# A streaming-encoder layer on one core: earlier input requests, squares folded further, memory operands and late taps moved in the engines' queues

## The reference

```
h = RMSNorm(x); split h @ w_in into q-latent, kv-latent, rope key, GLU input, gates A and B
yA = latent attention (16 heads, chunk-causal)        from the latents
yB = GLU -> causal depthwise conv, 31 taps -> LayerNorm -> swish -> @ w_pw2
x += (sigmoid(gA) * yA + sigmoid(gB) * yB) @ w_o
x += CrossAttn(RMSNorm(x), RMSNorm(mem))              4 heads, 256 memory tokens
x += SwiGLU(RMSNorm(x));  return RMSNorm(x)
```

## Time and profile before

| What | Value |
|---|---|
| timed runs, median (lowest to highest of 3) | 1681.59 us (1680.79 to 1682.99) |
| profiled execution, own time | 1683.29 us |
| its span, first to last instruction | 1681.1 us |
| TensorE busy | 1659.8 us, 99% |
| VectorE, ScalarE busy | 1111.0 and 826.2 us |
| mean granted TensorE clock | 0.997 |

### The profile page before, as it was taken

One profiled execution on the slowest core, in us unless ns is written; L12 is line 12 of the kernel. 1 busy time (PEld: TensorE's weight loads), 2 busy tenths in 40 slices (PEclk: granted clock), 3 DMA queues, 4 the chain that ended last, 5 costly groups with the idle time before them and its releaser, 6 DMA issues.

```text
span 1681.1 us, 23696 instructions
## 1 busy us (share of the span) xinstructions
PE 1659.8 (99%) x7728; PEld 1381.2 (82%) x7728; DVE 1111.0 (66%) x1414; ACT 826.2 (49%) x1049; POOL 102.0 (6%) x152
## 2 busy tenths in 40 slices
PE   8999999999999999999999999999999999999998
PEld 6888888888888888878888788888888888888886
DVE  5546777768987457885558856666666666654453
ACT  6555565555645444555544644444444444344343
POOL 3100010001000000120001200000000000000000
PEclk9999999999999999999999999999999999999999
DMA  6865555555665655554435566666666666565563
GB/s 209 260 200 163 175 157 164 153 166 159 183 212 182 197 191 175 181 192 157 150 133 174 189 196 193 191 186 187 196 200 198 190 193 193 189 223 188 176 213 136
DMA packets 160481, 309.67 MB, mean 184 GB/s; under 512 B 10256, under 2 KB 16400, under 8 KB 160176
## 3 DMA queue, kind: packets, MB, share of 16 engines
q1 hardware_dynamic: 158240, 301.50, 58.2%
q0 software_dynamic: 1488, 6.42, 1.1%
q10 hardware_dynamic: 704, 1.11, 0.2%
HBM read 306.89 MB, written 2.10 MB: 184 GB/s over the span
## 4 chain that ended last, share of the span: by engine, by line
PE 90%; DVE 4%; issue 3%; ACT 2%; DMA 1%; SPq 0%; DVEq 0%; ACTq 0%; POOLq 0%; POOL 0%
PE acc L357 27%; PE acc L359 27%; PE acc L358 27%; DVE w_lo L1247 2%; PE tp L369 1%; DVE x_f L1572 1%; ACT w_hi L772 1%; DMA raw<-in_w_in_dram 1%; PE acc L563 1%; PE acc L565 1%; PE sc L492 1%; PE acc L564 1%; PE ov L516 0%; PE sc L497 0%; PE acc L544 0%
## 5 line engine op out<-in xcount | busy, mean ns | idle before, releaser
L1247 DVE TENSOR_TENSOR w_lo<-raw,w_hi 128x1024 fp32r<-128x1024 f32 (+3 forms) x591 | 718.1, 1220 | 464.1 <-ACT w_hi L772 455.4
L772 ACT ACTIVATE w_hi<-raw 128x1024 fp32r<-128x1024 f32 (+3 forms) x591 | 606.0, 1027 | 764.3 <-PE acc L359 727.7
L357 PE MATMUL acc<-w_hi,crossT 128*128 128x512 f32 x832 | 325.1, 391 | 0.9 <-DVEq L1590 0.8
L358 PE MATMUL acc<-w_lo,crossT 128*128 128x512 f32 x832 | 323.9, 389 | 0.0
L359 PE MATMUL acc<-w_hi,crossT 128*128 128x512 f32 x832 | 323.9, 389 | 0.0
L357 PE MATMUL acc<-w_hi,mixT 128*128 128x512 f32 x796 | 316.4, 397 | 4.5 <-DVE w_lo L1247 2.2
L359 PE MATMUL acc<-w_hi,mixT 128*128 128x512 f32 x796 | 311.2, 391 | 0.0
L358 PE MATMUL acc<-w_lo,mixT 128*128 128x512 f32 x796 | 310.7, 390 | 0.0
L357 PEld LDWEIGHTS acc<-w_hi,crossT 128*128 128x128 f32 x832 | 156.2, 188 | 34.8 <-issue 1.6
L357 PEld LDWEIGHTS acc<-w_hi,mixT 128*128 128x128 f32 x796 | 150.0, 188 | 40.5 <-issue 6.9
L359 PEld LDWEIGHTS acc<-w_hi,crossT 128*128 128x128 f32 x832 | 156.2, 188 | 32.8
(11 more groups left out here) (251 smaller groups left out, 1405.1 us busy)
## 6 DMA issues: line engine op xcount, KB each, us to landing
raw<-in_w_in_dram SPq DMA_DIRECT2D x103, 512.0 KB, 3.8
raw<-in_w_gate_dram SPq DMA_DIRECT2D x88, 512.0 KB, 4.2
raw<-in_w_up_dram SPq DMA_DIRECT2D x88, 512.0 KB, 3.8
raw<-in_w_down_dram SPq DMA_DIRECT2D x80, 512.0 KB, 4.2
raw<-in_w_kv_mem_dram SPq DMA_DIRECT2D x64, 512.0 KB, 4.0
raw<-in_w_o_dram SPq DMA_DIRECT2D x32, 512.0 KB, 4.0
raw<-in_w_q_mem_dram SPq DMA_DIRECT2D x32, 512.0 KB, 3.7
raw<-in_w_o_mem_dram SPq DMA_DIRECT2D x32, 512.0 KB, 3.7
```

The lines of the kernel that those rows point to most:

```text
L357: mm(o, lo, whi, start=first and k == 0, stop=False)
L358: mm(o, hi, wlo, start=False, stop=False)
L772: fn(w_hi[:, s, 0:width], raw[:, s, 0:width], ACT.Copy).then_inc(hi_done, 1)
L1247: V.tensor_tensor(w_lo[:, s, 0:width], raw[:, s, 0:width], w_hi[:, s, 0:width].bitcast(F32), ALU.subtract).then_inc(lo_done, 1)
```

## The change

Seven edits, in the order of the lists:

1. SyncE requests x's blocks 12 to 15 together with blocks 8 to 11, before weight tile 4, no longer before tile 6.
2. `keep_busy` has 13 calls, not 17.
3. ScalarE rounds the first half of the first weight tile before x's operand 0, not behind it.
4. The squares are folded on to one block: two more adds (512 and 256 wide) in a third part of `fold_squares`. In stage A the parts come at iterations 2, 4 and 5 (they came at 2 and 5), for the memory tokens at iterations 3, 5 and 6 of the chunk (3 and 5). TensorE then has 2 products (4 passes), not 8 (16). ScalarE's groups of squares are spread otherwise: (0,1), (2), (3,4), (5,6), (7).
5. The memory operands 0 and 1 are made in iterations 9 and 11 of the last pair, and 2 to 7 in iterations 0 to 5 of stage E: two tiles ahead.
6. `late_taps` runs in chunks 1 to 4 of stage E.
7. The layer norm, its transposes and its activations come in chunk 5 of stage E.

```diff
@@ SyncE
             for t in range(16):
-                if t in (2, 4, 6):
-                    x_piece(2 * t, 2 * t + 4, x_in[t // 2])
+                if t == 2:
+                    x_piece(4, 8, x_in[1])
+                if t == 4:
+                    x_piece(8, 12, x_in[2])
+                    x_piece(12, 16, x_in[3])
@@ TensorE
-            keep_busy(17)
+            keep_busy(13)
             def add_squares(n):
                 pe.wait_ge(sq_added, n + 1)
                 for b in range(NB):
-                    for k in range(4):
-                        ins = mm(xt[:, b:b + 1], sqT[:, k, b * P:(b + 1) * P], ones[:, :], start=k == 0, stop=k == 3)
+                    ins = mm(xt[:, b:b + 1], sqT[:, 0, b * P:(b + 1) * P], ones[:, :], start=True, stop=True)
@@ TensorE, stage E: the norm's transposes move to chunk 5
+            for t in range(8):
+                products(T_E + 40, t, 8, mixT, 2 * t, 2, CH, C_E + 5)
                 if t == 1:
...
-            with pe.Fori(5, 8) as c:
+            with pe.Fori(6, 8) as c:
@@ ScalarE, start
+            act.wait_ge(raw_head, 16)
+            fn(w_hi[:, 0, 0:CH], raw[:, 0, 0:CH], ACT.Copy).then_inc(hi_head, 1)
             act.wait_ge(x_head, 16)
             operand_hi(0, "norm_mix")
-            act.wait_ge(raw_head, 16)
-            fn(w_hi[:, 0, 0:CH], raw[:, 0, 0:CH], ACT.Copy).then_inc(hi_head, 1)
...
+                if t == 3:
+                    act.wait_ge(x_in[3], 16)
...
-                for g in ((0, 1), (2, 3), (4,), (5,), (6, 7), (), (), ())[t]:
+                for g in ((0, 1), (2,), (3, 4), (5, 6), (7,), (), (), ())[t]:
                     squares(g)
@@ ScalarE, last pair; VectorE alike with operand_lo
-                    if last and t >= 8:
-                        operand_hi(t - 8, "norm_mem")
+                    if last and t in (9, 11):
+                        operand_hi(t // 2 - 4, "norm_mem")
@@ ScalarE, stage E, first chunk; VectorE alike
-                if t < 4:
-                    operand_hi(t + 4, "norm_mem")
+                if t < 6:
+                    operand_hi(t + 2, "norm_mem")
@@ VectorE, fold_squares
                     dve.wait_ge(sums_step, sums[0])
-                    V.tensor_tensor(sqT[:, 0:4, :], sqT[:, 0:4, :], sqT[:, 8:12, :], ALU.add).then_inc(sq_added, 1)
+                    V.tensor_tensor(sqT[:, 0:4, :], sqT[:, 0:4, :], sqT[:, 8:12, :], ALU.add).then_inc(sums_step, 1)
+                    sums[0] += 1
+                if part == 2:
+                    dve.wait_ge(sums_step, sums[0])
+                    V.tensor_tensor(sqT[:, 0:2, :], sqT[:, 0:2, :], sqT[:, 2:4, :], ALU.add).then_inc(sums_step, 1)
+                    sums[0] += 1
+                    dve.wait_ge(sums_step, sums[0])
+                    V.tensor_tensor(sqT[:, 0, :], sqT[:, 0, :], sqT[:, 1, :], ALU.add).then_inc(sq_added, 1)
...
-                if t == 2 or t == 5:
-                    fold_squares(0, t // 4)
+                if t in (2, 4, 5):
+                    fold_squares(0, (0, 1, 2)[(2, 4, 5).index(t)])
...
-                    if c == 3 and t in (3, 5):
-                        fold_squares(1, t // 4)
+                    if c == 3 and t in (3, 5, 6):
+                        fold_squares(1, (0, 1, 2)[(3, 5, 6).index(t)])
@@ VectorE, stage E
-                late_taps(0, t)
-            with dve.Fori(1, 4) as c:
+            with dve.Fori(1, 5) as c:
                 for t in range(8):
                     split_lo(c * 8 + T_E, t + 4)
-                    late_taps(c, t)
+                    late_taps(c - 1, t)
             for t in range(8):
-                split_lo(T_E + 32, t + 4)
+                split_lo(T_E + 40, t + 4)
```

More of the change, by code:

```diff
@@ L1038, in _ @@
                     keys_out(3, Q_K + 3)
+            for t in range(8):
+                if t == 7:
+                    values_out(1, C_E + 5, T_E + 48)
+                split_hi(T_E + 40, t + 4)
                 if t == 3:
@@ L1052, in _ @@
                             .then_inc(convT_hi, 1)
-            with act.Fori(5, 8) as c:
+            with act.Fori(6, 8) as c:
                 for t in range(8):
@@ L1300, in fold_squares @@
                     V.tensor_tensor(sqT[:, 0:4, :], sqT[:, 0:4, :], sqT[:, 4:8, :], ALU.add).then_inc(sums_step, 1)
-                else:
+                    sums[0] += 1
+                if part == 1:
                     dve.wait_ge(sq_done, 8 * n + 8)
                     V.tensor_tensor(sqT[:, 8:12, :], sqT[:, 8:12, :], sqT[:, 12:16, :], ALU.add).then_inc(sums_step, 1)
-                sums[0] += 1
-                if part == 1:
+                    sums[0] += 1
                     dve.wait_ge(sums_step, sums[0])
-                    V.tensor_tensor(sqT[:, 0:4, :], sqT[:, 0:4, :], sqT[:, 8:12, :], ALU.add).then_inc(sq_added, 1)
+                    V.tensor_tensor(sqT[:, 0:4, :], sqT[:, 0:4, :], sqT[:, 8:12, :], ALU.add).then_inc(sums_step, 1)
+                    sums[0] += 1
+                if part == 2:
+                    dve.wait_ge(sums_step, sums[0])
+                    V.tensor_tensor(sqT[:, 0:2, :], sqT[:, 0:2, :], sqT[:, 2:4, :], ALU.add).then_inc(sums_step, 1)
+                    sums[0] += 1
+                    dve.wait_ge(sums_step, sums[0])
+                    V.tensor_tensor(sqT[:, 0, :], sqT[:, 0, :], sqT[:, 1, :], ALU.add).then_inc(sq_added, 1)
             def mean_of_folded(n, norm):
@@ L1442, in gate_and_pair @@
                         attention(t, i - 1, i + (Q_C - 1))
-                    if last and t >= 8:
-                        operand_lo(t - 8, "norm_mem", G_MEM + t - 7)
+                    if last and t in (9, 11):
+                        operand_lo(t // 2 - 4, "norm_mem", G_MEM + t // 2 - 3)
                     at = share_first if first else share_last if last else share
@@ L1467, in _ @@
                 split_lo(T_E, t + 4)
-                if t < 4:
-                    operand_lo(t + 4, "norm_mem", G_MEM + t + 5)
+                if t < 6:
+                    operand_lo(t + 2, "norm_mem", G_MEM + t + 3)
                 if t == 2:
@@ L1508, in _ @@
                             .then_inc(convT_lo, 1)
-            with dve.Fori(5, 8) as c:
+            with dve.Fori(6, 8) as c:
                 for t in range(8):
```

## The result

The changed kernel takes 1685.61 us (median of 16 runs, 1684.20 to 1687.87), the kernel before 1682.55 us in the same session (16 runs, 1680.79 to 1683.52). Ratio 1.0020, 95% interval 1.0013 to 1.0027: a difference of 3.06 us, 0.18%. The forecast was 1684.3 against 1681.59, +2.7 us, range 1680.3 to 1688.8. The kernel is slower by more than sixteen runs of each leave uncertain, by an amount just inside the 0.2% that the prediction called "same". Its profiled execution has a span of 1683.8 us and a time of 1685.62, so 2.7 and 2.33 us more than the one of before.

A forecast was written before the change was run, and what follows sets the result against it. TensorE, busy 1659.8 of 1681.1 us, was taken as the bound, so only moved TensorE starts count. Terms -0.5 + 0.5 + 2.6, and 0.1 for a chunk start, gave +2.7: 1684.3 us, range 1680.3 to 1688.8.

The forecast's parts named there:

- Head: First 42 us: head products may start 0.6 us sooner, but tile 1 still waits for its weights; worth nothing.
- Requests: First 42 us: weight tile 4 lands up to 1.3 us later; ScalarE stalls 0.4 us, bounds 0 and 1.3.
- Fold in the first stage: First 42 us: sums at 33.2 instead of 31.82, but fewer passes; term -0.5 us, bounds -2.8 and +0.3.
- Second sums: At 147 us: the last two adds come behind VectorE's low part; term +0.5 us, bounds +0.2 and +0.8.
- Memory operands: 414 to 447 us: one ScalarE wait goes, operands come late for memory tiles; +2.6 us, bounds +1.2 and +3.3.
- Late taps: Stage E: moving late taps and layer norm is hidden by VectorE's slack; worth nothing, bound +0.9.
- Sum: Whole kernel: the terms and 0.1 for one more unrolled chunk start make +2.7 us, 1684.3 us.
- main case: Whole kernel: the terms come as forecast, 1684.3 us, own range 1682.5 to 1686.2; chance 0.46.
- B: Rival: granted clock falls at a new wait, before second sums or memory tile 1; +3.4 us, 1687.7; chance 0.22.
- C: Rival, first stage: tile 7 runs at 2.4 GHz; -2.4 us more, 1681.9; chance 0.16.
- D: Rival, memory stage: operands stay covered, operand 1 ready by 423.4; -3.5 us, 1680.8; chance 0.08.
- E: Rival, whole kernel: gains and waits within 1 us of each other, no effect, 1681.6; chance 0.08.

The follow-up runs named there:

- e7: Kernel before with only the start edits (x's last quarter requested earlier, 13 placeholder calls, first weight half rounded first): 1682.05 us, ratio 1.0000.
- before: The kernel without the seven edits: 1682.55 us beside the changed kernel; 1682.37, 1682.69 or 1681.54 us beside the follow-up kernels.
- e9: Kernel before with only the first stage's fold to one row: 1680.95 us, ratio 0.9996 to the kernel before.
- after: The changed kernel with all seven edits: 1685.61 us, ratio 1.0020 to the kernel before.
- e1: Changed kernel with only the memory operands put back as they were, four tiles ahead: 1681.97 us, ratio 1.0002 to the kernel before.
- e4: Changed kernel with the second fold's parts in iterations 3, 4 and 5, not 3, 5 and 6: 1683.57 us, ratio 1.0008 to the kernel before.
- e3: Kernel before with only the memory operands spread, two tiles ahead: 1685.46 us, ratio 1.0023.
- e2: Kernel before with only the late taps in chunks 1 to 4 and the layer norm in chunk 5: 1680.89 us, ratio 0.9994.
- e5: Changed kernel with TensorE's first sums behind tile 7 of stage A, not ahead of it: 1685.16 us, ratio 1.0018 to the kernel before.
- e8: Changed kernel with operands four tiles ahead, second fold earlier and first sums behind tile 7, together: 1679.61 us, ratio 0.9984 to the kernel before.
- e10: e8 with operand 7 made ahead of the first fold's second and third adds: 1679.66 us, ratio 0.9987 to the kernel before.
- e6: Changed kernel with 28 placeholder passes between tile 6 and the first sums: 1683.81 us, ratio 1.0012 to the kernel before.

## Why the prediction was right, step by step

**Head: right.** The head products started 0.6 us sooner, tile 1 at 12.28 for 12.14, and e7's time shows no gain.

**Requests: right in kind, too small.** A stall of 0.4 us was forecast, 0.62 came, and the sums moved by 0.75. The Trainium skill ("DMA: Bandwidth & Descriptors", Queues, rings and completion order) has descriptors consumed in ring order, by which the weights bear the whole 1.3 us of the prediction's estimate. The trace agrees: they landed 1.3 us later, not half of that. ScalarE lost less because in before they had landed 0.6 us ahead of its copy.

**Fold in the first stage: the delay right, the term not decided.** The sums came at 33.67, not 33.2, within the bounds of 32.7 and 33.9. The 1.15 us of two adds was right (32.47 to 33.61), and e9 has the sums 1.00 us later for the fold. What was low was the share of the requests: 0.75 us, where the forecast took part of 0.4. The term was forecast at -0.5 us; after's profile has +0.06 at 41.38 and -0.13 at 56.2. But e1 and e4, the same code, have -1.5 and -1.9 at 56.2, and e3 and e2, the start of before, -0.25 and -1.9. The means of three and three differ by 0.5 us, as forecast, with a spread of 2; a profile can't size this term, and e9's time (-0.6 us) has zero within its interval. The eleven slow products came in after's profile, the last ending at 39.7 with sums 0.47 us later than forecast, where 39.2 stood. That they were eleven is partly luck: e1 and e4 have eight.

**Second sums: right.** Start 148.55 (148.7 forecast), on at 149.01 (149.1), stage +0.54 (+0.5).

**Memory operands: right, in all three places.** Stage +2.7 from 319.9 to 441 us, forecast +2.6. The kv wait went, as said (416.74 for 416.55). Tile 0 came at 421.25, not 420.7: operand 0 on VectorE took 1.27 us, not 0.87, as the one at 420.18 in the earlier trace rows does; the forecast had the shorter duration although that row stood there. Tile 1 then waited 1.14, not 1.7, for both ran into the same chain, and began at 425.41 where 425.2 stood. Tile 5's wait was 0.54 for 0.7; tile 6 had none, though the shift grew by 0.2 us more up to its start.

**Late taps: right**, by e2 and by a ledger that is at +3.05 at 444 us and at +3.07 at 561.

**Sum.** -0.1, +0.5, +2.7 make +3.1 at 561 us; the profiles end 2.7 apart, since between 721 and 861 us small waits gave 0.3 back. That is no edit's doing: e9, which has none of the later edits, gains 0.4 us there against before. The medians differ by 3.06 for 2.7. Of the 1.3 us between 1685.61 and the forecast 1684.3, 1.0 is that the kernel before ran slower beside the changed one (1682.55 us for the 1681.59 of the forecast). The main case, given 0.46, was the one that came, and the time fell within its own range of 1682.5 to 1686.2. The stated range, 1680.3 to 1688.8, is wide enough to hold no change at all, so it is the places and not the range that speak for the mechanism.

**Rivals.** B did not come: 1.00 behind the waits of 1.62 and 1.52 us. The rule of the Trainium skill ("TensorE: Matmul & The Clock Gate", Why this matters for your kernels), no gaps above some 3 us, agrees for these. It does not cover the first stage, where after's own wait of 3.21 us is above it but others were not: low stretches came behind idle times of 2.13 (before), 1.80 (e5) and 2.60 us (e5, e8 and e10), while behind 1.84 us in e8 tile 7 ran at full speed. C did not come: an earlier stretch did fall where the wait hides it, at 12.3 us, and the later one came all the same. C's price was 2.4 us; e6 gives 1.9 against after's profile and 1.2 against those of e1 and e4. D falls with the three operand waits and e3. E falls with the interval of the ratio, 1.0013 to 1.0027.

## What to carry to other kernels

Count how long an operand takes through every engine that makes it, here 3.4 us, and hold it against the time of the tile that it is made behind, 2.7 us: two tiles ahead is then late wherever nothing else stands between tiles, and spreading work over later iterations makes it later. Fewer TensorE passes bought with more VectorE steps pay where the steps end before TensorE asks, and cost where they don't: the same fold lost 0.5 us at 147 us and won 1.3 there by standing one iteration sooner (e4). When a wait at a stage's end is taken away, follow the other chains to the next start first (sums, mean, row factor, copy): e5 and e10 removed a wait each and got nothing. And before two profiles of a start are compared, set them to the same zero, here the copy of the first whole weight tile: by the bare clock of the profile the earlier requests seemed to cost nothing, by that zero 0.75 us.

## What the runs showed of the hardware

A wait before a dense group can cost clock besides its own length. With 28 passes of no use across 3.3 us of idle TensorE the granted clock stayed at 1.00, and the tile behind took 3.3 us, where without them it took 4.4 (e1, e4) or 5.2 (after). The stretch at the 1.2 GHz level covered six to nine products of the same tile in three profiles of one code and eight to eleven in three of the other, and with the moment at which the first transfers land this makes single profiles of the stage differ by almost 2 us. 512 KB requested ahead of a weight tile made that tile land 1.3 us later, and the copy that needed it start 0.75 us later. Sixteen one-column passes took 1.70 us at the full clock and 3.15 where it fell among them; four took 0.46 at the full clock and 0.88 at the 1.2 GHz level.
